# One core, two blocks in sequence: the first tile's expert queries, keys and second choice ahead of the second tile's norm and queries

## What is computed

```python
def peer_ffn(h, w_q, sub_keys, peer_u, peer_v):
    ...
    def block(xb):
        q = jnp.einsum('td,de->te', xb, w_q).reshape(PEER_BLOCK, PEER_HEADS, 2, PEER_QDIM // 2)
        s = jnp.einsum('thpk,pnk->thpn', q, sub_keys).astype(jnp.float32)
        s_top, i_top = lax.top_k(s, PEER_TOPK)
        cand = (s_top[:, :, 0, :, None] + s_top[:, :, 1, None, :]).reshape(...)
        cand_idx = (i_top[:, :, 0, :, None] * PEER_NKEYS + i_top[:, :, 1, None, :]).reshape(...)
        g_top, pos = lax.top_k(cand, PEER_TOPK)
        expert = jnp.take_along_axis(cand_idx, pos, axis=-1)
        g = jax.nn.softmax(g_top, axis=-1)
        u = jnp.take(peer_u, expert, axis=0)
        act = jax.nn.gelu(jnp.einsum('thkd,td->thk', u, xb).astype(jnp.float32), approximate=False)
        vv = jnp.take(peer_v, expert, axis=0)
        return jnp.einsum('thk,thkd->td', (g * act).astype(xb.dtype), vv)
```

## Time and profile before

| | us |
|---|---|
| median of 3 runs | 2510.7 |
| lowest, highest | 2509.01, 2515.92 |
| the profiled execution | 2509.39 |
| its span | 2507.6 |
| PE, DVE, ACT, POOL busy in it | 2025.4, 1716.0, 973.5, 654.2 |
| first gather issued | 1080.43 |

### The profile page before, as it was taken

The page is one execution under the profiler, slowest core; times in us unless marked ns, Lnnn a source line. Parts: engine busy times, 40 slices in busy tenths (PEclk is TensorE's granted clock), DMA queues, the critical chain, the costliest instruction groups (busy, mean ns, idle before and its releaser), DMA issues.

```text
span 2507.6 us, 32141 instructions
## 1 busy us (share of the span) xinstructions
PE 2025.4 (81%) x11222; PEld 1322.8 (53%) x11222; DVE 1716.0 (68%) x3510; ACT 973.5 (39%) x2125; POOL 654.2 (26%) x631
## 2 busy tenths in 40 slices
PE   7999999999999999997765587877477868655555
PEld 6989898798989978764321132343122325211111
DVE  5787887777788776587588555558765757776454
ACT  4455443455544355433232224423224732322222
POOL 0000001010000100044344433334433434444442
PEclk9999999999999999998888798888788989787777
DMA  8635677674557754379999999999999999999998
GB/s 305 231 135 210 224 276 280 244 265 156 202 203 266 291 211 168 117 316 372 422 421 421 419 423 422 406 423 413 407 420 402 422 412 384 415 422 421 421 421 350
DMA packets 110940, 823.86 MB, mean 329 GB/s; under 512 B 14432, under 2 KB 15344, under 8 KB 31040
## 3 DMA queue, kind: packets, MB, share of 16 engines
q0 software_dynamic: 90000, 595.97, 58.5%
q1 hardware_dynamic: 20784, 225.89, 23.8%
HBM read 820.76 MB, written 1.05 MB: 328 GB/s over the span
## 4 chain that ended last, share of the span: by engine, by line
PE 47%; DMA 25%; DVE 12%; ACT 7%; issue 4%; POOL 2%; DVEq 1%; ACTq 1%; PEldq 0%; SPq 0%; POOLq 0%; PEld 0%
DMA ring_b<-in_peer_uv,eidx 17%; PE pd L658 14%; PE pr L1273 9%; PE pa L658 9%; PE pr L658 7%; DMA wring<-in_peer_uv,eidx 6%; DVE wring_r L1990 3%; DVE ring_b L2671 2%; PE pa L1296 2%; POOL ring_b L1930 2%; PE pa L1391 1%; ACT junk L1734 1%; DVE wring L2671 1%; PE pd L1296 1%; DMA wring<-in_w_mix 1%
## 5 line engine op out<-in xcount | busy, mean ns | idle before, releaser
L1273 PE MATMUL pr<-ring_b,junk 128*64 128x512 f32 x880 | 290.9, 769 | 171.5 <-ACT junk L1734 170.8
L1273 PE MATMUL pr<-wring,junk 128*64 128x512 f32 x840 | 277.1, 765 | 156.7 <-ACT junk L1734 156.2
L2671 DVE CUSTOM_DVE_ANT_0 ring_b<-ring_b,hrow 128x1024 f32<-128x1024 f32 x220 | 268.4, 1225 | 188.6 <-DMA ring_b<-in_peer_uv,eidx 182.0
L1930 POOL DMA_INDIRECT ring_b<-in_peer_uv,eidx x220 | 253.6, 1153 | 535.5 <-PE pr L1273 304.5
L2671 DVE CUSTOM_DVE_ANT_0 wring<-wring,hrow 128x1024 f32<-128x1024 f32 x210 | 256.1, 1224 | 186.4 <-DMA wring<-in_peer_uv,eidx 180.6
L1930 POOL DMA_INDIRECT wring<-in_peer_uv,eidx x210 | 241.8, 1151 | 341.1 <-PE pr L1273 282.3
L1724 ACT ACTIVATE gel<-dots 128x2 f32<-128x2 f32 x255 | 51.7, 203 | 629.5 <-DVE dots L2671 625.8
L1914 POOL DMA_DIRECT2D aring<-in_ada_rows x112 | 60.0, 535 | 826.2 <-DVE adal L2085 779.0
L1273 PEld LDWEIGHTS pr<-ring_b,junk 128*64 128x64 f32 x880 | 68.6, 163 | 359.6 <-ACT junk L1734 251.0
L1273 PEld LDWEIGHTS pr<-wring,junk 128*64 128x64 f32 x840 | 66.0, 163 | 338.8 <-ACT junk L1734 233.9
L1990 DVE TENSOR_TENSOR wring_r<-wring,wtop 128x2048 fp32r<-128x2048 f32 x76 | 171.7, 2262 | 65.0 <-ACT wtop L1436 63.3
(11 more groups left out here) (441 smaller groups left out, 4331.2 us busy)
## 6 DMA issues: line engine op xcount, KB each, us to landing
wring<-in_w_mix SPq DMA_DIRECT2D x38, 2048.0 KB, 8.7
aring<-in_ada_rows POOLq DMA_DIRECT2D x112, 512.0 KB, 5.9
wring<-in_w_ffn SPq DMA_DIRECT2D x22, 2048.0 KB, 8.8
wring<-in_w_lstm SPq DMA_DIRECT2D x12, 2048.0 KB, 8.2
wring<-in_w_stick SPq DMA_DIRECT2D x12, 2048.0 KB, 11.8
wring<-in_w_back SPq DMA_DIRECT2D x8, 2048.0 KB, 8.2
ring_c<-in_w_stick SPq DMA_DIRECT2D x5, 2048.0 KB, 12.6
wring<-in_w_back SPq DMA_DIRECT2D x4, 1536.0 KB, 6.5
```

Of the source, the lines that this page charges most:

```text
L1273: m = nc.tensor.matmul(pr[half][side, :], diag[:, p % DIAGS, :], row(p)[:, D + half * 512:D + (half + 1) * 512], start=p in FIRST_OF_SIDE, ...
L1930: pool.indirect_dma_start(out=row(q), out_offset=None, in_=ins["peer_uv"], in_offset=bass.IndirectOffsetOnAxis(ap=eidx[:, tt % NT, CHOSEN[ ...
L2671: m = nc.vector.tensor_tensor_reduce(out=row(q)[:, 0:D], in0=row(q)[:, 0:D], in1=hrow[:, q // PICKS % NT, SIDE[q], :], scale=1.0, scalar=0 ...
```

## The change

**The first tile's front.** DVE modulates four of the eight columns (`low_modulated`), ACT the other four (`high_modulated`). `first_queries` takes the first query block with its low columns ahead of its high ones, and stands between the halves of `out_rows(1, 14)`. `out_rows(1, 15)` and the second tile's gated sum, norm, transposes and modulation move behind the first tile's keys; the latter four behind the second choice, between picks 8 and 16. The gates of `dot` and of the first gather (`hrow_ready`, `late_rows`) are new waits.

**The picks' numbers.** `PLAN[0]`: the second choice has 8 dots in it (13 before), the third picks 16 to 41 (20 to 45), the fourth picks 72 to 122 (58 to 108). The second tile's sixteen query columns stand behind picks 10 to 54 and its `rows_back` behind 62 (40).

**The places.** Block 0 of the query weights is now needed until pick 16. Places 4 and 5 come in at pick 20 (6 before). The second tile's half of `hrow` is an eleventh place until pick 44.

```diff
-PLACES, IN_QUERIES, IN_WEIGHTS = 10, (6, 7), (8, 9)
-QUERIES_UNTIL, LENT, RETURNED = 32, 2 * PICKS - 8, 2 * PICKS + 98
+PLACES, IN_FIRST, IN_QUERIES, IN_WEIGHTS, SPARE = 11, (4, 5), (6, 7), (8, 9), (10,)
+FIRST_UNTIL, QUERIES_UNTIL, SPARE_UNTIL, LENT, RETURNED = 20, 32, 44, 2 * PICKS - 8, 2 * PICKS + 98
...
-    order, out = [0, 1, 2, 3, 8, 9, 4, 5], []
+    order, out = [0, 1, 2, 3, 8, 9] + list(SPARE), []
     for q in range(DEPTH * NT * PICKS):
+        if q == FIRST_UNTIL:
+            order = list(IN_FIRST) + order
         if q == QUERIES_UNTIL:
             order = list(IN_QUERIES) + order
+        if q == SPARE_UNTIL:
+            order = [r for r in order if r not in SPARE]
...
-EARLY_COLUMNS = {(0, 2): (0, 0, 2, 4), (0, 3): (8, 10, 14, 16), (1, 2): (18, 20, 20, 24), (1, 1): (28, 30, 32, 34), (1, 3): (42, 44, 46, 48)}
-ROWS_BACK, EARLY_KEYS, EARLY_GATES = 40, (50, 52, 54, 56), (60, 64)
+EARLY_COLUMNS = {(0, 2): (0, 0, 0, 2), (0, 3): (2, 4, 4, 6), (1, 0): (12, 14, 16, 18), (1, 2): (20, 22, 24, 26), (1, 1): (30, 34, 38, 42), (1, 3): (46, 50, 54, 58)}
+ROWS_BACK, EARLY_KEYS, EARLY_GATES = 62, (64, 66, 68, 70), (74, 78)
...
+                def first_queries():
+                    m = SLOTS_L
+                    pe.wait_ge(w_in_slot[place_of(m)], landed_b(m))
+                    b = bank_a()
+                    for k in range(KC):
+                        if k == 0:
+                            pe.wait_ge(thT_ready, 1)
+                        if k == FIRST_HALF:
+                            pe.wait_ge(high_columns, 1)
+                        for c in range(4):
...
-                out_rows(pr[3], 1, 14)
-                out_rows(pr[3], 1, 15)
+                out_rows(pr[3], 1, 14, range(KC // 4))
                 settle()
-                pe.wait_ge(thT_ready, 1)
-                queries(0, 0)
-                columns_of_tile(1)
+                first_queries()
+                out_rows(pr[3], 1, 14, range(KC // 4, KC // 2))
                 pe.wait_ge(experts_in, 32)
                 keys(0, 0)
                 queries(0, 1)
+                out_rows(pr[3], 1, 15)
+                settle()
+                keys(0, 1)
                 rows_back(0)
-                keys(0, 1)
-                pe.wait_ge(thT_ready, 2)
-                queries(1, 0)
                 divided_queries(0, 2)
                 keys(0, 2)
                 divided_queries(0, 3)
                 keys(0, 3)
-                divided_queries(1, 2)
-                divided_queries(1, 1)
+                weighted(0, PLAN[0]["part", len(CHOICE_WORK) - 1], False)
+                columns_of_tile(1)
+                weighted(0, PLAN[0]["summed"], False)
+                pe.wait_ge(thT_ready, 2)
+                pe.wait_ge(high_columns, 2)
+                for j in (0, 2, 1):
+                    divided_queries(1, j)
+                divided_queries(1, 3)
                 weighted(0, ROWS_BACK, False)
                 rows_back(1)
-                divided_queries(1, 3)
...
             def experts_first():
-                for t in range(NT):
-                    tile_squares(t, mixed, True)
+                tile_squares(0, mixed, True)
+                high_modulated(0)
...
                 key(0, 3)
...
+                gelus(0, PLAN[0]["part", len(CHOICE_WORK) - 1])
+                tile_squares(1, mixed)
+                gelus(0, PLAN[0]["summed"])
+                high_modulated(1)
+                divided_query(1, 0)
...
+            pool.wait_ge(late_rows, 2)
...
             choose(0, 0)
             choose(1, 0, spread_over(0, "part"))
+            late_gated(1)
+            gated_sum(1, mixed)
+            picks(0, PLAN[0]["summed"])
+            tile_normed(1, 1)
+            picks(0, PLAN[0]["normed"])
+            low_modulated(1)
             picks(0, PLAN[0]["between"])
             choose(2, 0, spread_over(0, "rest"))
```

More of the change, by code:

```diff
@@ L190 @@
 STICK_BEFORE = [0, len(STICK_GROUPS[0])]
-PLAN = [counted(0, choice("part", 13, 1, sum(CHOICE_WORK) // 4) + [("between", 7)] + choice("rest", 25) + [("late", 13)] + choice("choose", 50)),
+PLAN = [counted(0, choice("part", 8, 1, sum(CHOICE_WORK) // 4) + [("summed", 2), ("normed", 2), ("between", 4)] + choice("rest", 25) + [("late", 31)] + choice("choose", 50)),
         plan_of(0), plan_of(1), counted(0, [("first", 2)] + choice("late", 40))]
@@ L484, in build @@
         tss_ready, txn_ready, thT_ready = sem("tss_ready"), sem("txn_ready"), sem("thT_ready")
+        high_columns = sem("high_columns")
+        hrow_ready = sem("hrow_ready")
         mixed, experts_done, stick_done = sem("mixed"), sem("experts_done"), sem("stick_done")
@@ L1065, in queries @@
                         after_column(c)
+                def first_queries():
[8 more added lines that the diff above has]
+                        for c in range(4):
+                            i = mm(b[:, c * P:(c + 1) * P], place(m)[:, k, c * P:(c + 1) * P], hT[:, k, 0:P],
+                                   k == 0 and c == 0, k == KC - 1 and c == 3)
+                    i.then_inc(pa_full, 1)
                 def keys(t, q4):
@@ L1069, in keys, with out_rows @@
                     key_bank(lambda hp, cut: qp[t][:, hp, cut], q4)
-                def out_rows(b, t, m):
+                def out_rows(b, t, m, ks=range(KC // 2)):
                     if t == 0:
@@ L1075, in out_rows @@
                     i = rows_product(b, of_lstm(m), tile_of(y_hi, t), tile_of(y_lo, t),
-                                     lambda k: k % 4 == 0 and pe.wait_ge(yT_ready, 2 * t + k // 4 + 1))
+                                     lambda k: k % 4 == 0 and pe.wait_ge(yT_ready, 2 * t + k // 4 + 1), ks)
+                    if KC // 2 - 1 not in ks:
+                        return
                     if t:
@@ L1626, in flat, with high_modulated @@
                 return v.rearrange("p c n -> p (c n)")
+            def high_modulated(t):
+                u = DEPTH * D_UNITS + 4 + 4 + 4 + 2 + 2 * t + 1
+                act.wait_ge(pd_full, u + 1)
+                for i in range(4):
+                    c = FIRST_HALF + i
+                    m = nc.scalar.activation(hT[:, c, t * P:(t + 1) * P], pd[u % 2][:, i * P:(i + 1) * P], ACT.Identity,
+                                             scale=modA[:, 1, c:c + 1], bias=adac[:, 3 * KC + c:3 * KC + c + 1])
+                m.then_inc(pd_free, 1)
+                act.drain().then_inc(high_columns, 1)
             def experts_first():
-                for t in range(NT):
-                    tile_squares(t, mixed, True)
+                tile_squares(0, mixed, True)
+                high_modulated(0)
                 def query(t, j):
@@ L1638, in key, with divided_query @@
                     act.drain().then_inc(sc_ready, 1)
+                def divided_query(t, j):
+                    c = EARLY_COLUMNS[t, j]
+                    gelus(0, c[2])
+                    gelus(0, c[3])
+                    query(t, j)
                 query(0, 0)
@@ L1643, in experts_first @@
                 exponents(0, 0, *CHOICES[0][0][1:])
+                key(0, 1)
                 rows_back(0)
-                key(0, 1)
-                query(1, 0)
-                gelus(0, EARLY_COLUMNS[0, 2][2])
-                query(0, 2)
-                gelus(0, EARLY_COLUMNS[0, 2][3])
+                divided_query(0, 2)
                 key(0, 2)
@@ L1693, in rows_back @@
                         nc.scalar.copy(hrow[:, t, s, half * 512:(half + 1) * 512], take()).then_inc(pa_free, 1)
+                act.drain().then_inc(hrow_ready, 1)
             def exponents(n, t, h0, h1):
@@ L2556, in _, with low_modulated, late_gated @@
             gated_sum(0, mixed)
-            tile_normed(0, 0, True)
-            tile_modulated([(1, hT[:, :, 0:P])])
-            for half in range(2):
+            def low_modulated(t):
+                b = take()
+                nd[0] += 1
+                for c in range(FIRST_HALF):
+                    nc.vector.tensor_scalar(hT[:, c, t * P:(t + 1) * P], b[:, c * P:(c + 1) * P], modA[:, 1, c:c + 1], shift(1)[:, c:c + 1],
+                                            ALU.mult, ALU.add)
+                dve.drain()
+                dve.sem_inc(pd_free, 1)
+                dve.sem_inc(thT_ready, 1)
+            def late_gated(half):
                 c = slice(half * 512, (half + 1) * 512)
@@ L2668, in dot @@
             def dot(q):
+                if q % PICKS == 0:
+                    dve.wait_ge(hrow_ready, q // PICKS + 1)
                 dve.wait_ge(row_in[ROW[q]], 16 * TURN[q])
```

27 lines of the change are left out of this document (12 added, 15 removed).

## The result

The changed kernel takes 2521.12 us, the median of 20 executions (2512.32 to 2526.49). The kernel before, run beside it, takes 2511.44 (20 executions, 2506.76 to 2524.90). The ratio, estimated from all the executions, is 1.0035, with a 95% interval of 1.0027 to 1.0044: 8.8 us slower, where +5.0 was forecast. It is not the quotient of the two medians, which would be 1.0039, 9.7 us. The profiled execution took 2518.18 us, with a span of 2516.3.

The account below looks back on a forecast made before the run. From the first gather on, the DMA's bytes, that gather's time and DMA losses set the end. Front gain, moved load and gather 20's late place, with slow products, sum to +5.0 us: 2515.7 on the median, range 2507 to 2522.

Parts of the forecast that it names:

- the sum: All terms up to gather 20 taken together: +5.0 us, with bounds of +3.4 and +8.4.
- The front: First tile's start: shorter modulation and fewer products ahead bring the first choice 4.8 us earlier, first gather at 1075.7.
- line: Landing time of pick k less 2.485 k; constant while the DMA is full; forecast 1100.5 from gather 20, against 1095.5.
- The head start: The first choice, and so the first gather, comes earlier by 4.8 us.
- The gate at pick 20: Gather 20 waits for the last column of the second tile's first query block on PE; issued at 1143.7.
- The clock: Slower PE products after a gap: 1.6 us charged once, for the wait before picks 0 and 1.
- the rival: PE's gaps before gather 20 each cost 1.7 us, or slowness lasts longer: +7 to +11, 2518 to 2522; chance 0.22.
- three gaps of 1.7 on +3.4: Upper bound: slow PE products after each of three gaps, each in full, given as +8.4.
- What else moves, and costs nothing: Later gathers, second to fourth choices and new waits shift without cost; gather 128 needed just when the fourth choice ends.
- The 3.57 us at the third choice: DVE's wait for keys in the kernel before, said to go because the third choice's keys are there long before.
- the fourth choice is late: Rival: gather 128 waits for the fourth choice's end, needing a 10 us slip; +1 to +5 more; chance 0.03.
- the one for "wrong": Signs against the forecast: gather 20 before 1139, line rising again between picks 21 and 130, or first gather after 1077.

Follow-up runs that it names:

- places26: The changed kernel with places 4 and 5 coming in at pick 26 instead of 20; 2514.96 us, ratio 1.0014 to the kernel before.
- warm: The changed kernel with 26 idle identity products on PE in its wait ahead of picks 0 and 1; 2519.91 us, ratio 1.0034 to the kernel before.
- late37: The changed kernel with the fourth choice from pick 78 instead of 72, in 44 dots instead of 50; 2516.07 us, ratio 1.0017 to the kernel before.
- both: The changed kernel with places 4 and 5 from pick 26 and the fourth choice from pick 78; 2510.88 us, ratio 0.9997 to the kernel before.

## Why the prediction was right, and where not

The time lies in the range, and its sign was the forecast's. Of +8.8, the sum had +5.0: one of two losses was foreseen, and the other was not. That 2521.12 is inside 2507 to 2522 owes as much to the width of the range as to the sum; it is outside the 2512 to 2518 that had a chance of 0.50.

- **The front was right.** `first_queries` started at 1054.04 (1053.4 was said), `keys(0, 0)` at 1062.75 (1062.1), the first gather at 1076.32 (1075.7). Over the eight traces that share this front it lies between 1074.5 and 1079.0, on average 1076.8; over the four with the old front, the choice was done at 1081.4 on average. The head start is 4.7 us; 4.8 was said.
- **The gate at pick 20 was right.** Issue at 1144.52 (1143.7), line 1100.8 (1100.5), with the DMA at 169 GB/s from 1140 to 1150. `places26` shows that this one gate costs 5.3 us. Between picks 24 and 28 the line rose by 1.4 more; the sum had 1.0 until pick 46, as before.
- **The clock was mis-sized.** I charged 1.6 us of slow products once; it was 2.7 at picks 0 and 1, and 1.7 more at picks 6 and 7 (5.35 us for eight products where 3.65 are usual), these beside DVE's norm, which ended at 1119.9 anyway. The Trainium skill, page "TensorE: Matmul & The Clock Gate", section "What's actually happening", says that PE is throttled until activity releases it, and the trace agrees, with the granted 0.50. As it was told, with full gaps on the way to gather 20, the rival was wrong: gather 20 went out 0.8 us behind the time of the sum, and `warm` takes the dearer of the two slow phases away and leaves the time. But its 2518 to 2522 was the right band, and the clock did have a part in the second loss, where all three turns of the ring ran their products at 0.51 to 0.53. How much of the time that is stays open. Two of its numbers also had no ground: three gaps of 1.7 on +3.4 make +8.5, not 8.4, and no row led to the +11.
- **"What else moves, and costs nothing" is the step that failed.** I asked of the fourth choice whether it would end in time, and it did. I didn't ask whether its keys would be there when it began. All that was needed stood in the change: `rows_back` behind pick 62, keys behind 64, 66, 68 and 70, the choice from pick 72, so the last keys two picks ahead of it, while PE runs several picks behind DVE. In the kernel before the distance was the same (keys behind 56, the choice from 58) and the wait 4.37 us; there `rows_back` stood ten picks ahead of the keys, where it now stands two ahead, and PE reached them late. No run separates that from the slow turns. The 3.57 us at the third choice were a warning of the same wait, and I only booked them as a gain. It cost 4.5 us (`late37`), and the rival that came near it, "the fourth choice is late", had the wrong end of it, 0.03 of chance and "+1 to +5".
- Of the signs named beforehand, the one for "wrong" came true: the line rose again between picks 21 and 130. The sign was drawn too wide, since the rise of about 10 where other loads share the DMA stands in both kernels; the 5.8 between picks 71 and 93 are what it should have named.

With this term the sum is +9.5, and 8.8 was measured. What the part of the change that is left brings is seen in `both`: −0.8 us, with an interval of −3.0 to +1.5.

## What to carry to other kernels

Where a queue issues strictly in order, a resource that comes free late must not have an early turn: two places that came in at pick 20 cost 5.3 us, and at pick 26 no gather waited for them. When a block of work is moved in a plan, look at its inputs as much as at its deadline: count how far the engine that makes them runs behind the engine that reads them. And try the parts of a change alone: the eleventh place, put on the old kernel, made it 0.22% faster (0.12% in a second kernel with a later fourth choice), while in the new order no gain from it could be measured.
